# A hybrid convolution and S5 block: another order of the input projections, DRAM round trips by quarters, another opening

## What is computed

```python
h = rmsnorm(x, norm1_g) * (1.0 + sc1) + sh1          # x: 2048 x 1024, modulation from c
u_conv, u_ssm, gl_conv, gl_ssm = split(h @ w_in)     # 2*512, 512, 1024, 1024 columns
y_conv = conformer_conv(u_conv, ...)                 # a*sigmoid(g), causal depthwise conv of 31 taps,
                                                     # layernorm, silu, @ conv_proj
y_ssm = s5_mixer(u_ssm, ...)                         # 32 groups of 16 channels, 64 complex states, scan
                                                     # over time, gelu, @ ssm_glu, za * sigmoid(zb)
merged = sigmoid(gl_conv) * y_conv + sigmoid(gl_ssm) * y_ssm
x = x + g1 * (merged @ w_out)
h = rmsnorm(x, norm2_g) * (1.0 + sc2) + sh2
x = x + g2 * ((silu(f_gate) * f_up) @ w_ffn_out)     # f_gate, f_up from h @ w_ffn_in
return rmsnorm(x, final_g)
```

## Time and profile before

| | us |
|---|---|
| runs | 2675.8, 2668.9, 2676.42; median 2675.8 |
| the profiled execution | 2679.86 |
| its span, first to last instruction | 2678.1 |
| TensorE busy | 2567.8 (96%) |
| GpSimd busy | 1821.0 (68%) |
| VectorE busy | 1504.9 (56%) |
| ScalarE busy | 725.4 (27%) |

### The profile page before, as it was taken

How to read it: one execution, slowest core, us unless ns; L and a number is a source line. 1 busy time by engine, 2 the same in 40 slices (tenths; PEclk the granted TensorE clock), 3 DMA queues, 4 the chain that set the end, 5 groups by cost and what they waited for, 6 DMA issues and landing times.

```text
span 2678.1 us, 30702 instructions
## 1 busy us (share of the span) xinstructions
PE 2567.8 (96%) x11675; PEld 2112.9 (79%) x11675; DVE 1504.9 (56%) x1782; ACT 725.4 (27%) x1120; POOL 1821.0 (68%) x1204
## 2 busy tenths in 40 slices
PE   6889999999999899989899999999999999999997
PEld 3778787878888788877788888878888878888886
DVE  4999733986299745987633334463333325544631
ACT  3212321133112321135333345443333322111100
POOL 2656675686776677665687777787777756666664
PEclk8999998999999999999999999999999999999999
DMA  8776347653765348562232232322323256655532
GB/s 266 183 183 187 112 162 153 173 184 103 213 169 183 114 145 203 151 204 87 94 103 87 81 116 73 112 84 71 95 71 95 73 196 205 196 163 181 173 134 71
DMA packets 420026, 378.29 MB, mean 141 GB/s; under 512 B 88024, under 2 KB 326312, under 8 KB 419752
## 3 DMA queue, kind: packets, MB, share of 16 engines
q1 hardware_dynamic: 321440, 299.48, 37.0%
q10 hardware_dynamic: 98440, 76.85, 10.3%
HBM read 312.11 MB, written 55.71 MB: 137 GB/s over the span
## 4 chain that ended last, share of the span: by engine, by line
PE 65%; DVE 25%; DMA 4%; issue 2%; ACT 2%; ACTq 1%; POOL 1%; DVEq 0%; POOLq 0%
PE bank L1546 13%; PE bank L1547 13%; PE bank L1548 13%; DVE bank L753 11%; PE bank L1777 6%; PE bank L1775 6%; PE bank L1776 6%; PE bank L1692 2%; PE bank L1694 2%; PE bank L1693 2%; DVE wst L809 1%; DVE bank L787 1%; DMA hraw<-hid_scratch 1%; DVE wst L789 1%; DMA u<-us_scratch 1%
## 5 line engine op out<-in xcount | busy, mean ns | idle before, releaser
L1845 POOL TENSOR_TENSOR w_lo<-raw,w_hi 128x1024 fp32r<-128x1024 f32 x192 | 484.0, 2521 | 15.4
L1843 POOL CAST w_hi<-raw 128x1024 fp32r<-128x1024 f32 x192 | 213.6, 1113 | 410.5 <-PE bank L1548 322.5
L1546 PE MATMUL bank<-h_hi,w_hi 128*128 128x512 f32 x896 | 354.6, 396 | 8.4 <-ACT sg_c L1185 6.5
L1547 PE MATMUL bank<-h_lo,w_hi 128*128 128x512 f32 x896 | 351.2, 392 | 0.0
L1548 PE MATMUL bank<-h_hi,w_lo 128*128 128x512 f32 x896 | 351.0, 392 | 0.0
L753 DVE SCALAR_TENSOR_TENSOR bank<-uc,cwt,bank 128x512 f32<-128x512 f32 x464 | 328.4, 751 | 8.0
L1868 POOL TENSOR_TENSOR fw_lo<-fsum,fw_hi 128x512 fp32r<-128x512 f32 x176 | 234.0, 1331 | 106.9 <-ACT fw_hi L1336 106.9
L1546 PE MATMUL bank<-xc_hi_T,fw_hi 128*128 128x512 f32 x704 | 276.6, 393 | 8.7 <-DVE tr L937 6.3
L1775 PE MATMUL bank<-ow_hi,hid_hi 128*128 128x512 f32 x704 | 274.7, 390 | 3.6 <-DVE hid_lo L997 3.6
L1548 PE MATMUL bank<-xc_hi_T,fw_lo 128*128 128x512 f32 x704 | 275.1, 391 | 0.0
L1547 PE MATMUL bank<-xc_lo_T,fw_hi 128*128 128x512 f32 x704 | 275.0, 391 | 0.0
(11 more groups left out here) (301 smaller groups left out, 5163.4 us busy)
## 6 DMA issues: line engine op xcount, KB each, us to landing
raw<-in_w_in SPq DMA_DIRECT2D x112, 512.0 KB, 4.7
raw<-in_w_ffn_in SPq DMA_DIRECT2D x66, 512.0 KB, 5.3
raw<-in_w_ffn_out SPq DMA_DIRECT2D x66, 512.0 KB, 4.5
hid_scratch<-tr SPq DMA_DIRECT2D x88, 256.0 KB, 2.5
hraw<-hid_scratch SPq DMA_DIRECT2D x88, 256.0 KB, 3.8
g2b<-in_w_ada SPq DMA_DIRECT2D x64, 256.0 KB, 4.2
ssm_m<-vk_scratch SPq DMA_DIRECT2D x32, 512.0 KB, 4.8
raw<-in_ssm_glu SPq DMA_DIRECT2D x32, 512.0 KB, 3.5
```

The lines of the kernel that those rows point to most:

```text
L1546: t.matmul(dst, wh, xh, start=first, stop=False)
L1547: t.matmul(dst, wh, xl, start=False, stop=False)
L1843: g.tensor_copy(hi[:], src[:]).then_inc(hi_done, 1)
L1845: g.tensor_tensor(lo[:], src[:], hi[:].bitcast(F32), ALU.subtract).then_inc(split_done, 1)
```

## The change

In the later blocks the order becomes conv tile 0, us0 and us1, conv tile 1, us2 and us3, conv tile 2, S0-3, conv tile 3, gl0-7, then Y0..3. VectorE does tiles 0 and 1 whole ahead of the rotations. Both trips through DRAM are split by quarters, with a semaphore for each: eight DMAs of 32 KB for a quarter, in all four times as many. Two gates are evicted between the exchanges. `PIECE_AT` and `ahead` are moved by a few chunks. In block 0 conv tile 1 comes ahead of the state matrix, the eight kernel stores are put between the exchanges, and in the prologue the 32 transposes of `nat_b` move from ahead of the second slab product to behind the fourth turned tile, and VectorE's angles move.

```diff
@@ -79,15 +79,19 @@
 
     o_ssm, o_gl = 2 * CW, 2 * CW + SW
 
-    WEIGHT_CHUNKS = [("in", o_ssm + m * P) for m in range(KS)]
-    for m in range(KC):
-        WEIGHT_CHUNKS += [("in", m * P), ("in", CW + m * P)]
-    WEIGHT_CHUNKS += [("in", o_gl + i * P) for i in range(2 * KD)]
+
+    conv_chunks = [[("in", m * P), ("in", CW + m * P)] for m in range(KC)]
+    ssm_chunks = [("in", o_ssm + m * P) for m in range(KS)]
+    FIRST_CHUNKS = [ssm_chunks + sum(conv_chunks, [])]
+    FIRST_CHUNKS += [conv_chunks[0] + ssm_chunks[0:2] + conv_chunks[1] + ssm_chunks[2:4] + conv_chunks[2]
+                     + conv_chunks[3]] * (NB - 1)
+    WEIGHT_CHUNKS = [("in", o_gl + i * P) for i in range(2 * KD)]
     for p in range(KD // 2):
         WEIGHT_CHUNKS += [("glu", 2 * p * P), ("glu", D + 2 * p * P)]
     WEIGHT_CHUNKS += [("proj", 2 * p * P) for p in range(KD // 2)]
     WEIGHT_CHUNKS += [("out", h, j) for h in range(2) for j in range(KD // 2)]
-    NW = len(WEIGHT_CHUNKS)
+    WEIGHT_CHUNKS = [first + WEIGHT_CHUNKS for first in FIRST_CHUNKS]
+    NW = len(WEIGHT_CHUNKS[0])
...
             at = [(part - 1, w) for w in range(38, NW)]
-            at += [(part, w) for w in range(1, 10)] + [(part, w) for w in range(18, 33)]
+            at += [(part, w) for w in range(1, 11)] + [(part, w) for w in range(21, 35)]
...
-        nat_b = early(h_at, tr_at, ("nat_b0", [G, 2, NST, HG]), ("nat_b1", [G, 2, NST, HG]))
+        nat_b = early(tr_at, tr_at + 16384, ("nat_b0", [G, 2, NST, HG]), ("nat_b1", [G, 2, NST, HG]))
...
-        GY, GE = [7, 5, 5, 5], [12, 11, 11, 11]
+        GY, GE = [7, 8, 8, 8], [12, 13, 13, 13]
...
             if b == 0:
-                names += conv_in(0) + [f"wt{n}" for n in R(8)] + ["ct0", "ct1"] + conv_in(1, 2, 3)
+                names = ssm_in_(*R(KS)) + conv_in(0, 1) + [f"wt{n}" for n in R(8)] + ["ct0", "ct1"] + conv_in(2, 3)
                 names += [f"kk{n}" for n in R(8)] + quarters
             else:
-                names += conv_in(0, 1) + quarters + conv_in(2, 3)
+                names = conv_in(0) + ssm_in_(0, 1) + conv_in(1) + ssm_in_(2, 3) + conv_in(2) + quarters + conv_in(3)
...
-        pe_pro = ["v1", "ada1", "bx", "ada3", "v0", "ada5", "ada7", "sums", "mt"] + h_steps + ["v2"]
+        pe_pro = ["v1", "ada1", "ada3", "v0", "ada5", "ada7", "sums", "mt"] + h_steps[0:4] + ["bx"] + h_steps[4:] + ["v2"]
...
-        CONV = [tile_taps(0, 0, 13), tile_taps(0, 13, 20), tile_taps(0, 20) + tile_taps(1) + [tm for t in R(TAPS) for tm in ((t, 2), (t, 3))]]
-        taps = lambda part: [f"c{t}_{m}" for t, m in CONV[part]]
+        tiles_23 = [tm for t in R(TAPS) for tm in ((t, 2), (t, 3))]
+        CONV = [[tile_taps(0, 0, 13), tile_taps(0, 13, 20), tile_taps(0, 20) + tile_taps(1) + tiles_23]]
+        CONV += [[tile_taps(0), tile_taps(1), tiles_23]] * (NB - 1)
...
+            dve.wait_ge(*scal.after("pro", "dt"))
+            link(v.tensor_tensor(lg, dt, ar, ALU.mult))
+            link(v.tensor_tensor(jexp[:], iota_f[:, 0:T + 1].unsqueeze(2).broadcast_to([P, T + 1, G]),
+                                 lg.unsqueeze(1).broadcast_to([P, T + 1, G]), ALU.mult))
+            link(v.tensor_tensor(th, dt, ai, ALU.mult))
+            reduce_angle(th, th, t0)
...
-            dve.wait_ge(*scal.after("pro", "dt"))
-            link(v.tensor_tensor(lg, dt, ar, ALU.mult))
-            link(v.tensor_tensor(jexp[:], iota_f[:, 0:T + 1].unsqueeze(2).broadcast_to([P, T + 1, G]),
-                                 lg.unsqueeze(1).broadcast_to([P, T + 1, G]), ALU.mult))
-            link(v.tensor_tensor(th, dt, ai, ALU.mult))
-            h_split("pro", 0)
-            reduce_angle(th, th, t0)
-            h_split("pro", 1)
-            h_split("pro", 2)
+            for k in R(5):
+                h_split("pro", k)
             angles(jarg[:, 0, :, :], jarg[:, 1, :, :], jtmp[:], th, T + 1, "jargs")
-            for k in R(3, KD):
+            for k in R(5, KD):
                 h_split("pro", k)
 
...
             gated(0, 0)
+            gated(0, 1)
...
             for j in R(4):
                 output_matrix(j)
-            gated(0, 1)
+            gated(0, 2)
             for j in R(4, T + 1):
                 output_matrix(j)
-            gated(0, 2)
...
                     gated(b, 1)
                     conv(1)
+                    gated(b, 2)
...
-                    if b and q % 2:
-                        gated(b, 2 + q // 2)
+                    if b and q == 1:
+                        gated(b, 3)
...
-            def store_kernel():
+            def store_kernel(*steps):
...
-                for m in R(KS):
-
+                def ssm_input(m):
                     act.wait_ge(*tensor.after(b, f"us{m}"))
                     s.activation(uz[:, m, :, :].rearrange("p s c -> p c s"),
                                  bank[plan[b, f"us{m}"]][:].rearrange("p (c s) -> p c s", s=T), ACT.Copy)\
                         .then_inc(*scal.step(b, f"us{m}"))
                     act.wait_ge(*scal.after(b, f"us{m}"))
-                    act.dma_start(us_d[m * P:(m + 1) * P], uz[:, m, :, :]).then_inc(uz_out, 16)
-                act.wait_ge(uz_out, 64 * (b + 1))
-                for t in R(T):
-                    act.dma_start(u8[t * HG:(t + 1) * HG, :, :], us_d[:, t, :].rearrange("(g h) c -> h g c", h=HG))\
-                        .then_inc(u8_in, 16)
+                    act.dma_start(us_d[m * P:(m + 1) * P], uz[:, m, :, :]).then_inc(uz_out[m], 16)
+
+                def ssm_turn(m):
+                    act.wait_ge(uz_out[m], 16 * (b + 1))
+                    for t in R(T):
+                        act.dma_start(u8[t * HG:(t + 1) * HG, m * GT:(m + 1) * GT, :],
+                                      us_d[m * P:(m + 1) * P, t, :].rearrange("(g h) c -> h g c", h=HG))\
+                            .then_inc(u8_in[m], 16)
+
...
                 if b == 0:
+                    ssm_input(0)
+                    ssm_input(1)
+                    ssm_turn(0)
+                    ssm_input(2)
+                    ssm_turn(1)
+                    ssm_input(3)
+                    ssm_turn(2)
+                    ssm_turn(3)
                     sigmoid_u(0)
+                    sigmoid_u(1)
                     state_matrix()
                     rotation_tables()
-                    for m in R(1, KC):
-                        sigmoid_u(m)
+                    sigmoid_u(2)
+                    sigmoid_u(3)
                     kernel_tiles()
                 else:
                     sigmoid_u(0)
+                    ssm_input(0)
+                    ssm_input(1)
+                    ssm_turn(0)
+                    ssm_turn(1)
                     sigmoid_u(1)
+                    ssm_input(2)
+                    ssm_input(3)
+                    ssm_turn(2)
+                    ssm_turn(3)
+                    sigmoid_u(2)
...
-                if b == 0:
-                    store_kernel()
-                else:
-                    sigmoid_u(2)
+                early_gates = 2
                 for q in R(NQ):
-                    if b and q == 2:
+                    if b == 0:
+                        store_kernel(2 * q, 2 * q + 1)
+                    elif q == 1:
                         sigmoid_u(3)
+                    if q >= 2:
+                        gate(q - 2)
                     act.wait_ge(*vec.after(b, f"sc{q}"))
                     exchange(dt_[q][:], wst[:, q * GQ:(q + 1) * GQ, 0:NC], turned_in[q])
                 act.wait_ge(*vec.after(b, "last"))
                 exchange(ctmp[:], carry[:], carry_in)
-                for i in R(GY[b]):
+                for i in R(early_gates, GY[b]):
                     gate(i)
+
+                def load_output(m):
+                    act.wait_ge(y_out[m], 16 * T * (b + 1))
+                    act.dma_start(yz[:, m, :, :], ys_d[m * P:(m + 1) * P]).then_inc(yz_in[m], 16)
+
                 for q in R(NQ):
                     act.wait_ge(*tensor.after(b, f"Y{q}"))
                     s.activation(u8[:, q * GQ:(q + 1) * GQ, :], bank[plan[b, f"Y{q}"]][:]
                                  .rearrange("p (g k) -> p g k", g=GQ), ACT.Copy).then_inc(*scal.step(b, f"Y{q}"))
-                    if q == NQ - 1:
-                        act.wait_ge(*scal.after(b, f"Y{q}"))
-                        for t in R(T):
-                            act.dma_start(ys_d[:, t, :].rearrange("(g h) c -> h g c", h=HG),
-                                          u8[t * HG:(t + 1) * HG, :, :]).then_inc(y_out, 16)
+                    act.wait_ge(*scal.after(b, f"Y{q}"))
+                    for t in R(T):
+                        act.dma_start(ys_d[q * P:(q + 1) * P, t, :].rearrange("(g h) c -> h g c", h=HG),
+                                      u8[t * HG:(t + 1) * HG, q * GQ:(q + 1) * GQ, :]).then_inc(y_out[q], 16)
+                    if q:
+                        load_output(q - 1)
                     gate(GY[b] + q)
-                act.wait_ge(y_out, 16 * T * (b + 1))
```

(28 more changed lines are left out.)

39 lines of the change are left out of this document (20 added, 19 removed).

## The result

The changed kernel takes 2656.5 us in the median (2652.3 to 2657.9), the one before 2677.5 in the same comparison; the ratio is 0.9914 (95% interval 0.9894 to 0.9935). The forecast was 2641 with a range of 2630 to 2658. The sign is right and the time is in the range, 15.5 us above the likeliest value: of a forecast gain of 35 us some 21 came.

A forecast was written before the change was run, and what follows sets the result against it. TensorE, busy 2567.8 of 2678.1 us, was taken as the bound, with its waits and low clock as the gain. 35 us from the later blocks plus 0 from block 0, off the median 2675.8, gave 2641; range 2630 to 2658.

The forecast's parts named there:

- The later blocks: Blocks 1 to 3: savings of 15.3, 9.7 and 11.4 us, together 36.4, taken as 35 after 1.4 for small new waits.
- `Ds3`: Rotations in the later blocks: it ends at B+110.5 to B+116.2, ahead of TensorE's need at B+116.7, so no wait.
- about 292: Sign for the later blocks: about 292 us each from start to start.
- the 15.3 us of block 1: Gain in block 1: 5.8 and 0.9 us of waits, 6.7 and 1.9 us from the clock.
- Block 0: Prologue and block 0: 3.7 us gained, set against late ug2 (1.7) and GpSimd beside tables and first rotation (some 2): net 0.
- opening: Prologue: with the transposes of `nat_b` out of the way, up to 4.3 us shorter, taken as 3.7.
- the bound of +7: Upper bound for block 0: +7 us if its second rotation runs at the pace of block 2.
- block 0 grows: Rival for block 0: a slower second rotation adds 7 us or less, giving 2645 to 2650; chance 0.11.
- a wait of za of 8 to 13 us in block 0: Sign at za in block 0: TensorE waits 8 to 13 us for `ys_lo` there, and not in the later blocks.
- The wait for gl6's chunk: Block 0, behind the kernel stores: gl6 may wait up to 9 us, which costs nothing by itself.
- The issue queue: Rival at the later blocks' input trips: 32 KB DMAs at 1.01 us each make S3 wait, 2683 to 2700; chance 0.06.
- the third rival: The same rival as "block 0 grows": 2645 to 2650, chance 0.11.

The follow-up runs named there:

- before_again: The kernel before, profiled and timed once more with nothing changed: 2678.0 us, ratio 0.9998.
- e7: The kernel before with only the opening changed (transposes of `nat_b` behind the fourth tile of h, VectorE's pole arithmetic ahead of its wait for the sums): 2675.3 us.
- e10: The kernel before with only the middle of block 0 in the changed kernel's order (ua1 and ug1 ahead of the state matrix): 2686.8 us, ratio 1.0033.
- e3_row: The changed kernel with block 0's eight kernel stores issued in one row and gates 0 and 1 evicted behind the exchanges: 2650.9 us, ratio 0.9906.
- e5_in_whole: The changed kernel with the input trip of blocks 1 to 3 in one piece, eight DMAs of 128 KB behind the last input store: 2707.6 us, ratio 1.0106.
- e6_out_whole: The changed kernel with the output trip of blocks 1 to 3 in one piece, eight stores of 128 KB behind Y3: 2656.6 us, ratio 0.9928.

## Why the prediction was right, and where it was off

**The later blocks** held point by point: -37.8 against a sum of 36.4 worked out and 35 taken. In block 1 the gated tile ended at B+12.4 (12.3), S0 had no wait, the issues took 0.49 (0.51), `Ds3` was within its bounds, the GELUs 5 us ahead of za. The last quarter landed at B+54.5 there and at B+57.4 and B+57.2 in blocks 2 and 3 (57, needed by 60). Block 3 takes 298.1 us and not the "about 292" of the signs; the prediction's own sum, 309.9 less 11.4, has it right. One thing I had wrong: the 15.3 us of block 1 were partly chance. In before_again its S0 waits 2.6 us instead of 5.8, while block 2, where the earlier trace rows shows no wait, has one of 1.9, and the two blocks take 302.6 and 303.7 us instead of 308.0 and 302.1. Over the four profiles with the old later blocks whole (before, before_again, e7, e10) the three took 915.8 to 920.1, so the lasting gain is 33 to 38, and a term read from the one profile was at the upper end of it.

**Block 0** is the step that failed, by its size: "GpSimd now works beside the tables and the first rotation, some 2 us". The mechanism was named and then taken at a quarter of its size. In the trace VectorE has: opening -3.8 (forecast -3.7), tables +7.6, ug2 late +1.7 (1.7), the second rotation and carry +2.7 (in the bound of +7, not in the sum), 0.5 in small ones, less 0.8 on the halo copy: +7.9 at `ys_lo`, +8.4 at block 1. That is 1.4 above the upper bound of +7, which left the tables out altogether. I had the earlier trace rows with 1.11 against 3.25 beside me, but priced only the rotations with it. The case "block 0 grows" was a rival of 0.11, with the wrong member of the family.

The Trainium skill (SBUF — State Buffer, Who interferes with whom) had the missing point a little below the rule that I quoted: besides instructions with two SBUF inputs, `tensor_scalar` and copies can run in a mode that takes the shared port too. The trace agrees: the single-input `ktmp` operation went from 1.24 to 3.28 us. Had I gone through the tables with that rule, all 13 operations would have been candidates, against two GpSimd chunks of 3.5 us and their pieces.

**The signpost** "a wait of za of 8 to 13 us in block 0" came in at 10.1 though the step behind it was off: TensorE and VectorE were both late. A wait is a difference of two arrivals and doesn't show either; the start of block 1 (388 to 396 said, 401.0 seen) was the sign that told. The wait for gl6's chunk (8.8, forecast up to 9) cost nothing by itself within 1 to 2 us: in e3_row TensorE lost more at that place and za started earlier.

**The issue queue**, the rival on the other side, did not come: its tip was at 0.70 us an issue, and the rows of sixteen took 0.49 to 0.60. e5_in_whole shows that its mechanism, S0 late and then at a low clock, is real and would have made the kernel slower; only its condition was not met.

**Outside the sum** stood the FFN. Taking its length from a single profile as a constant is good to some 4 us in this kernel, and the same holds for the step from a span to a median: the profiled run of before was 4.1 us above its median, that of after (2657.7) is 1.2 above. The books close: 2641 + 8.4 for block 0 - 2.8 for the later blocks + 7.2 for the FFN + 2.9 for the two medians is 2656.7. Of the 15.5 us between the forecast and the result, 8.4 are a cost that I priced wrongly and 10.1 (7.2 and 2.9) are of the size by which profiles and runs of one kernel differ, less the 2.8 that the later blocks gave beyond the sum. Block 0 alone would have given 2649, within the third rival's 2645 to 2650 though by another cause; the rest stands in no term of the sum. That the range held the result, by 1.5 us, is in part luck.

## What to carry to other kernels

When a change lets one engine run on where it used to stand, list what the engines beside it do at that very time: the idle stretch was cover for somebody. Price contention for every operation in the stretch, not for the kind that the last profile happened to show slowed: each can lose what is left of the other engine's operation when it begins. And compare kernels by landmarks inside the trace, each stage from its own first instruction, before a difference of spans is explained.

## What the runs showed of the hardware

- A VectorE operation on a 128x32 tile took 0.18 to 0.19 us alone and 0.95 to 2.27 us when it began beside a running GpSimd operation; wide ones (128x2080) went from 1.24 to 3.28 and from 2.33 to 3.27. A slowed operation ended with GpSimd's (98.48 against 98.44) or up to its own length behind it, and one that began first kept its time (0.19 at 95.99). GpSimd pays as well: its cast took 2.66 us there and 1.04 elsewhere. Small operations lose most in proportion: the six narrow ones went from 1.3 to 5.2 us together.
- The same race of two engines makes a stretch in which nothing was changed vary: TensorE's wait for `hid_lo` was 0.5 to 0.9, 2.1 to 2.3 or 4.6 us in the 14 profiles, by how many of two VectorE operations began ahead of GpSimd's cast.
- A DMA of 32 KB cost ScalarE's queue 0.49 us to issue in a row of sixteen (7.83 us; 0.60 in the slowest row), as much as one of 128 KB while its queue isn't full (0.51). Sixteen small ones carried two quarters in time where eight large ones (8.12 us) stalled. The Trainium skill (DMA: Bandwidth & Descriptors, Measured) asks for DMAs of 1 MiB or more. No run here sets one size against the other at the same start; for a trip that is judged by when its last piece lands, e5_in_whole is 52.5 us slower in the three blocks with pieces four times as large, which can't start before all four stores have landed.
- What a wait does to the clock behind it isn't a matter of its length alone: at the same place, for `m_lo` at the end of block 3, a wait of 1.9 us had a stretch of 3.4 us at 0.50 (1.2 GHz) behind it in e6_out_whole and a granted clock of 1.00 in the changed kernel.
